# A gated tile moved ahead of the combined activation blocks, and the low half of one weight tile made by VectorE

## The chip, the core and the metric

The kernel runs on one core of a Trainium2 chip. Its time is the device time in microseconds (us) of one execution; less is better. Five engines run side by side: TensorE (PE) multiplies matrices, VectorE (DVE) and ScalarE (ACT) work on tiles, GpSimd (POOL) and SyncE (SP) mostly issue transfers. They keep step by semaphores: an instruction waits until a counter has reached a value, and adds to a counter when it ends. Each engine works through its own list in order.

## The reference

Two layers of an encoder; a token matrix of 512 tokens and 1024 features passes a convolution branch and a state-space branch, is merged and normalised to `h`, and then goes through a gated feed-forward part. The change stands in that part of each layer:

```
h = layer_norm(DEEPNORM_ALPHA * x + merged @ w_o[i], ln1_g[i], ln1_b[i])
g_, u_ = jnp.split(h @ w_gate_up[i], 2, axis=-1)
h2 = layer_norm(DEEPNORM_ALPHA * h + (jax.nn.silu(g_) * u_) @ w_down[i], ln2_g[i], ln2_b[i])
```

`w_gate_up` has 2 x 2816 columns, that is 22 pairs of a gate tile and an up tile of 128 columns; `w_down` brings the 2816 features back to 1024, that is 8 output tiles, each summed over 22 tiles of 128 rows.

## The kernel before

**Two halves of every operand.** Weights and activations are float32. TensorE takes them as a rounded high half and a low half, the rest, and forms three products per tile: high by high, high by low, low by high (`three`, lines 1090 to 1094). `xh` and `xl` (x_hi, x_lo) are the halves of the activations that a stage multiplies, `aah` and `aal` (act_a_hi, act_a_lo) those of the gated tiles 0 to 7, `abh` and `abl` those of the tiles 8 to 15.

**Weight cycles and slots.** Most weights come from one stream in cycles of four tiles of 128x1024, one for each slot (`SLOTS` = 4). A weight tile goes through these steps. SP loads it into one of two raw buffers (`tile`, line 412): slots 0 and 2 share one, slots 1 and 3 the other, so a load waits for `hi_done` of the slot that used the buffer last. ScalarE (`hi`, line 578) copies it to `w_hi`, which rounds it, and writes it with the sign turned to `w_lo`. GpSimd (`lo`, line 469) waits for `hi_done` and issues a transfer that adds the same weights from memory onto `w_lo`, which leaves the weights less the rounded weights, the low half. TensorE (`dense`, line 1100) waits in `slot_ready` for `lo_done` of the slot and for the bank to be free (`evac`), multiplies eight tiles of 128 rows, three products each, into the bank of the slot, and signals `used`. SP, ScalarE and GpSimd handle the tiles in the order of the stream.

**The feed-forward part.** Gated tiles 0 to 3 (`WHOLE` = 4) are made from whole weight tiles, in the two cycles that begin at `C_UP0`: slots 0 and 1 are gate and up of one tile, slots 2 and 3 of the next. For such a tile ScalarE takes the gate's bank with Silu into `sg` (sigmoids), VectorE multiplies it with the up bank into `u` (`swish`, line 2128), ScalarE rounds that into `aah`, VectorE writes the rest into `aal` (`low_act`, line 2136). Tiles 4 to 15 (`UNITS` = 12) are made from 7 smaller products each (`product`, line 1457), a scheme with sums and differences of quarter blocks. It needs four combined blocks of the activations: VectorE forms differences of quarters of the normalised activations (`combine`, line 2072), ScalarE rounds them (`combined_hi`, line 909), VectorE writes the rest (`combined_low`, line 2076). Their weights come from a second array, `w_units`, which SP loads into `z_a` and the raw buffers (`units`, line 417) as soon as the combined blocks have been read out of `z_a` (`t_done`). VectorE and ScalarE make sums of them, and a ring of quarter slots, rounded by ScalarE and completed by GpSimd, holds the rest. Seven products in the order P1, P2, P4, P6, P5, P3, P7 make one tile.

Then the first down cycle (`C_DOWN0`) follows, the whole weight tiles for the down product over gated tiles 0 to 7. Its four tiles are rounded while the last of the 12 units is still being multiplied: ScalarE's `frame` (line 946) calls `hi` for slot 0 behind that unit's first product, and for slots 1 to 3 behind its products P4, P5 and P7.

**Order around the first place.** ScalarE first writes the eight normalised activation tiles (line 906), then rounds the four combined blocks (lines 977 and 978), and then starts gated tile 0 with Silu (line 983) and the two weight tiles of the following cycle. VectorE forms the four differences and the four low halves (lines 2084 to 2092) and then starts `swish` of tile 0 (line 2142 on).

Of the kernel before, what the change touches and what calls it, by code (L numbers as in the profile page):

```python
# [152 lines left out]
def build(nc, x_in, p_in, w_stream, w_units, w_dt, w_ple, par_in, out):  # L153
    ctx = ExitStack()
    with ctx:
# [231 lines left out]
        out_done = sem("out_done")  # L387
        g1_done = sem("g1_done")
# [22 lines left out]
        def _(sp):  # L411
# [36 lines left out]
            for L in range(LAYERS):  # L448
                for first, end, n in ((0 if L else 1, C_DOWN0, WT), (C_DOWN0, C_DOWN2, WT), (C_DOWN2, C_PLE, LAST * P),
                                      (C_PLE, CYCLES, WT)):  # L450
                    if first == C_DOWN0:
                        units(L)
                    with sp.Fori(L * CYCLES + first, L * CYCLES + end) as cyc:
                        for s in range(SLOTS):
                            tile(cyc, s, n)
# [10 lines left out]
        def _(gp):  # L466
# [60 lines left out]
            with gp.Fori(0, LAYERS) as L:  # L527
# [30 lines left out]
                for first, end, n in ((C_GATE_A, C_DOWN0, WT), (C_DOWN0, C_DOWN2, WT), (C_DOWN2, C_PLE, LAST * P), (C_PLE, CYCLES, WT)):  # L558
# [8 lines left out]
                    with gp.Fori(first + (first == C_GATE_A), end) as c:  # L567
# [4 lines left out]
        def _(act):  # L572
# [235 lines left out]
            for L in range(LAYERS):  # L808
# [137 lines left out]
                def frame(n):  # L946
# [3 lines left out]
                    if n < UNITS:  # L950
# [7 lines left out]
                        else:  # L958
                            hi(on(post, C_DOWN0), 0)
# [17 lines left out]
                for i in range(4):  # L977
                    combined_hi(i)
                for f in range(WHOLE):
# [11 lines left out]
                    if not last:  # L991
                        hi(on(c, 1), 2 * r + 1)
                    elif r == 0:
# [92 lines left out]
        def _(pe):  # L1086
# [8 lines left out]

            def slot_ready(cyc, s):
                pe.wait_ge(lo_done[s], 16 * (cyc[0] + 1))
# [14 lines left out]
            def projection(cyc, m, ks=range(4)):  # L1112

                s, h, b = m // 2, m % 2, m % SLOTS
                if ks[0] == 0:
                    pe.wait_ge(lo_done[s], 16 * (cyc[0] + 1))
# [281 lines left out]
            for L in range(LAYERS):  # L1398
# [99 lines left out]
                pe.wait_ge(fl_done, seen(FT * L + KT))  # L1498
                phase(post, C_DOWN0, C_UP2, aah, aal, ready=lambda m: None,
# [25 lines left out]
        def _(dve):  # L1525
            open_(dve, xl_done, dtw_lo, dt_v, ad_ready, turn_ready, grp_ready, conv_done, cb_done,
# [330 lines left out]
            with dve.Fori(0, LAYERS) as L:  # L1857
# [226 lines left out]
                dve.wait_ge(zf_ready, seen(2 * KT * (L + 1)))  # L2084
                combine(0, quadrant(0, 1), quadrant(0, 0))
                dve.wait_ge(t_ready, seen(4 * L + 1))
                combine(1, quadrant(1, 1), combined_sum(0))
                combine(2, quadrant(1, 1), quadrant(0, 1))
                dve.wait_ge(t_ready, seen(4 * L + 2))
                combine(3, quadrant(1, 0), combined_sum(1))  # L2090
                for i in range(4):
                    combined_low(i)

# [48 lines left out]
                for f_ in range(WHOLE):  # L2142
# [32 lines left out]
                for n in range(UNITS + 1):  # L2175
# [13 lines left out]
                    if n > 0:  # L2189
                        low_act(WHOLE + n - 1)  # L2190
                    if n < UNITS:
# [157 lines left out]
```

## Time and profile before

| | |
|---|---|
| median of 3 runs | 2382.52 us (2378.63 to 2385.85) |
| profiled execution | 2385.37 us, its span 2383.5 us |
| TensorE busy | 2328.1 us, 98% of the span |
| VectorE, ScalarE busy | 1666.2 us (70%), 1415.3 us (59%) |
| transfers, share of the 16 DMA engines | 46.4% issued by GpSimd (adding onto `w_lo`), 26.0% issued by SP |
| granted TensorE clock, mean | 0.994 of full speed |

The span runs from the first to the last instruction. Matmuls are pipelined, so TensorE counts as busy while one still drains; a new one starts each 0.23 us with 512 columns at full clock, though each is listed with 0.39 us. A wait is listed with the engine or transfer that ended it. The two layers run the same program: what layer one does near 800 us, layer two does near 1983.

### The profile page before, as it was taken

Reading aid. Unit: us, or ns where it says so; the run is one execution under the profiler, and the core shown is the slowest. Engines: PE = TensorE matmul, PEld = TensorE weight load, DVE = VectorE, ACT = ScalarE, POOL = GpSimd, SP = SyncE. Lnnn points to the kernel's source line nnn. Section 1 sums busy time; section 2 is a strip of 40 time slices with the busy share of each in tenths; the row PEclk is TensorE's granted clock in tenths of the full one; section 3 lists DMA queues with packets and bytes.
Section 4 is the critical chain, followed back from the end, with each engine's and each line's share of the span. In section 5 each row is a group of like instructions: output and inputs, shape, how many; then the busy total and the mean of one; then the engine's idle time right before and its main releaser. Section 6 shows DMA issues by size and latency. Waiting matters only on the chain.

```text
span 2383.5 us, 37119 instructions
## 1 busy us (share of the span) xinstructions
PE 2328.1 (98%) x12312; PEld 1967.9 (83%) x12312; DVE 1666.2 (70%) x2964; ACT 1415.3 (59%) x2439; POOL 493.7 (21%) x581
## 2 busy tenths in 40 slices
PE   8999999999999899999999999999999998999999
PEld 6878888887877799888788888888878777998886
DVE  4899898989545487213758999989895464871147
ACT  5756657376565676444657566664656655763446
POOL 2222222222111122111112122223311111221110
PEclk9999999999999999999999999999999999999999
DMA  7677575857878577988775857747588876778985
GB/s 205 142 167 152 126 176 118 183 131 162 182 182 197 143 182 160 200 205 188 160 160 121 183 126 165 171 108 173 127 177 177 187 184 155 186 166 197 213 188 137
DMA packets 115738, 396.90 MB, mean 167 GB/s; under 512 B 12784, under 2 KB 12784, under 8 KB 115568
## 3 DMA queue, kind: packets, MB, share of 16 engines
q0 software_dynamic: 57600, 188.77, 46.4%
q1 hardware_dynamic: 55728, 200.56, 26.0%
q10 hardware_dynamic: 2240, 5.42, 0.6%
q8 instruction: 93, 1.52, 0.3%
q14 instruction: 77, 0.63, 0.1%
HBM read 392.60 MB, written 2.10 MB: 166 GB/s over the span
## 4 chain that ended last, share of the span: by engine, by line
PE 78%; ACT 8%; DVE 7%; DMA 3%; issue 3%; POOL 1%; POOLq 0%; DVEq 0%; SPq 0%; ACTq 0%
PE bank L1092 21%; PE bank L1094 21%; PE bank L1093 21%; DMA w_lo<-w_stream 3%; PE bank L1134 2%; PE bank L1135 2%; PE bank L1137 2%; ACT decay L635 2%; PE bank L1211 1%; ACT w_lo L584 1%; ACT w_hi L583 1%; PE bank L1217 1%; DVE tmp_m L1657 1%; ACT y_hi L656 1%; PE bank L1229 1%
## 5 line engine op out<-in xcount | busy, mean ns | idle before, releaser
L1092 PE MATMUL bank<-x_hi,w_hi 128*128 128x512 f32 (+1 forms) x1632 | 621.2, 381 | 18.8 <-DMA w_lo<-w_stream 18.8
L1094 PE MATMUL bank<-x_hi,w_lo 128*128 128x512 f32 (+1 forms) x1632 | 608.1, 373 | 0.0
L1093 PE MATMUL bank<-x_lo,w_hi 128*128 128x512 f32 (+1 forms) x1632 | 607.5, 372 | 0.0
L474 POOL DMA_DIRECT2D w_lo<-w_stream x328 | 281.6, 858 | 1438.4 <-ACT w_lo L584 1376.4
L583 ACT ACTIVATE w_hi<-w_raw 128x1024 fp32r<-128x1024 f32 (+1 forms) x330 | 350.1, 1061 | 284.9 <-PE bank L1094 246.0
L1092 PEld LDWEIGHTS bank<-x_hi,w_hi 128*128 128x128 f32 x1632 | 309.4, 190 | 74.0 <-DMA w_lo<-w_stream 20.4
L1094 PEld LDWEIGHTS bank<-x_hi,w_lo 128*128 128x128 f32 x1632 | 309.1, 189 | 54.6
L1093 PEld LDWEIGHTS bank<-x_lo,w_hi 128*128 128x128 f32 x1632 | 309.6, 190 | 53.5 <-issue 3.3
L584 ACT ACTIVATE w_lo<-w_raw 128x1024 fp32r<-128x1024 f32 (+1 forms) x330 | 347.4, 1053 | 0.0
L1570 DVE SCALAR_TENSOR_TENSOR z_a<-glu_out,params,z_a 128x497 f32<-128x497 f32 (+14 forms) x480 | 321.0, 747 | 0.0
L1092 PE MATMUL bank<-act_a_hi,w_hi 128*128 128x512 f32 x480 | 190.2, 396 | 7.8 <-DMA w_lo<-w_stream 4.5
L1094 PE MATMUL bank<-act_a_hi,w_lo 128*128 128x512 f32 x480 | 187.6, 391 | 0.0
L1093 PE MATMUL bank<-act_a_lo,w_hi 128*128 128x512 f32 x480 | 187.5, 391 | 0.0
L1570 DVE SCALAR_TENSOR_TENSOR xs_b_c<-conv_in,params,xs_b_c 128x510 f32<-128x510 f32 (+1 forms) x256 | 184.2, 790 | 0.0
L1134 PE MATMUL bank<-w_hi,x_hi 128*128 128x256 f32 x512 | 153.0, 299 | 1.6 <-DMA w_lo<-w_stream 1.2
L483 POOL TENSOR_SCALAR_AFFINE_SELECT seg_rhs<-steps_split 128x512 fp32r<-128x512 f32 x128 | 130.4, 1099 | 94.7 <-PE bank L1181 94.7
L1135 PE MATMUL bank<-w_lo,x_hi 128*128 128x256 f32 x512 | 144.8, 283 | 0.0
L1137 PE MATMUL bank<-w_hi,x_lo 128*128 128x256 f32 x496 | 140.4, 283 | 0.0
L635 ACT ACTIVATE decay<-bank,steps 128x64 f32<-128x64 f32 x512 | 115.0, 407 | 0.2
L1092 PEld LDWEIGHTS bank<-act_a_hi,w_hi 128*128 128x128 f32 x480 | 90.5, 189 | 29.4 <-DVE act_a_lo L1713 4.1
L651 ACT ACTIVATE squares<-y_tok 128x257 f32<-128x257 f32 x64 | 26.8, 419 | 135.7 <-DVE y_tok L1691 135.7
L1093 PEld LDWEIGHTS bank<-act_a_lo,w_hi 128*128 128x128 f32 x480 | 90.4, 188 | 20.0 <-issue 1.4
(302 smaller groups left out, 4537.3 us busy)
## 6 DMA issues: line engine op xcount, KB each, us to landing
w_raw<-w_stream SPq DMA_DIRECT2D x314, 512.0 KB, 5.1
w_lo<-w_stream POOLq DMA_DIRECT2D x312, 512.0 KB, 7.6
w_lo<-w_units POOLq DMA_DIRECT2D x72, 256.0 KB, 5.3
z_a<-w_units SPq DMA_DIRECT2D x32, 512.0 KB, 4.5
w_raw<-w_units SPq DMA_DIRECT2D x16, 512.0 KB, 4.5
w_raw<-w_stream SPq DMA_DIRECT2D x16, 384.0 KB, 3.8
w_lo<-w_stream POOLq DMA_DIRECT2D x16, 384.0 KB, 6.2
z_b<-x_in SPq DMA_DIRECT2D x4, 512.0 KB, 6.2
```

Of the source, the lines that this page charges most:

```text
L474: gp.dma_start(wlo[:, s, 0:n], w_stream[cyc, s, :, 0:n].bitcast(F32R), accum_op=ALU.add).then_inc(lo_done[s], 16)
L483: gp.affine_select(out=rhs[:, part], in_=ad, compare_op=ALU.is_ge, fill=0.0, base=-1, pattern=[[0, 2 * HG], [-2, HB]], channel_multiplier= ...
L583: act.activation(whi[:, s, 0:n], raw[:, s % 2, 0:n], ACT.Copy)
L584: act.activation(wlo[:, s, 0:n], raw[:, s % 2, 0:n], ACT.Copy, scale=-1.0).then_inc(hi_done[s], 1)
L635: i = act.activation(E[:, c, h, t], quarters(bank[4 + c % 2])[:, h, t], ACT.Exp, bias=of(EDGE, half, c, g)[:, h:h + 1])
L1092: pe.matmul(dst, wh, mh, start=first, stop=False)
L1093: pe.matmul(dst, wh, ml, start=False, stop=False)
L1094: return pe.matmul(dst, wl, mh, start=False, stop=last)
L1134: pe.matmul(dst, xh[:, k, t], h, start=k == 0, stop=False)
L1135: pe.matmul(dst, xh[:, k, t], l, start=False, stop=False)
L1137: pe.matmul(dst, xl[:, k, t], h, start=False, stop=end)
L1570: q = dve.scalar_tensor_tensor(out=outs[i][:, a:b], in0=ins[i][:, a + o:b + o], scalar=w[:, k:k + 1], in1=outs[i][:, a:b], op0=ALU.mult, o ...
```

## The change

Two edits. The first moves work in the order of ScalarE and VectorE. On VectorE `swish` of gated tile 0 stands ahead of the four combined blocks, and its `low_act` between their differences and their low halves. On ScalarE the Silu of gated tile 0, its rounding and the weight tiles of slots 0 and 1 of the next cycle stand ahead of the rounding of the combined blocks. The second takes slot 0 of the first down cycle out of the usual path: ScalarE only writes `w_hi`, and VectorE subtracts it from the raw weights into `w_lo` and signals the new semaphore `low_by_vector`. GpSimd issues no transfer for that slot, SP loads slot 2 of that cycle only after the signal, since it overwrites the raw buffer that VectorE reads, and TensorE waits for the signal and counts one transfer less on slot 0 from there on (`vector_made`). The diff (the line that opens the semaphore for VectorE is left out):

```diff
@@ -385,6 +385,7 @@
         product_done = sem("product_done")
         kept = sem("kept")
         out_done = sem("out_done")
+        low_by_vector = sem("low_by_vector")
         g1_done = sem("g1_done")
         g2_done = sem("g2_done")
         u_ready = sem("u_ready")
@@ -450,7 +451,13 @@
                                       (C_PLE, CYCLES, WT)):
                     if first == C_DOWN0:
                         units(L)
-                    with sp.Fori(L * CYCLES + first, L * CYCLES + end) as cyc:
+                        cyc = L * CYCLES + C_DOWN0
+                        tile(cyc, 0)
+                        tile(cyc, 1)
+                        sp.wait_ge(low_by_vector, seen(L + 1))
+                        tile(cyc, 2)
+                        tile(cyc, 3)
+                    with sp.Fori(L * CYCLES + first + (first == C_DOWN0), L * CYCLES + end) as cyc:
                         for s in range(SLOTS):
                             tile(cyc, s, n)
             tile(ALL_CYCLES, 0)
@@ -564,7 +571,8 @@
                             t, h = {"P1": (1, 0), "P2": (1, 1), "P4": (0, 1)}[p]
                             gp.dma_start(part(wlo, q), w_units[L * UNITS + u_, t, :, h * HALF:(h + 1) * HALF].bitcast(F32R),
                                          accum_op=ALU.add).then_inc(ring_lo[q], 16)
-                    with gp.Fori(first + (first == C_GATE_A), end) as c:
+                        lo(base + C_DOWN0, 1, 2, 3)
+                    with gp.Fori(first + (first in (C_GATE_A, C_DOWN0)), end) as c:
                         lo(base + c, 0, 1, 2, 3, n=n)
 
 
@@ -956,7 +964,9 @@
                             ringed(n + 1, "P2")
                             ringed(n + 1, "P4")
                         else:
-                            hi(on(post, C_DOWN0), 0)
+                            act.wait_ge(raw_ready[0], (base[0] + C_DOWN0 + 1) * 16)
+                            act.wait_ge(used[0], seen(post[1] + C_DOWN0))
+                            act.activation(whi[:, 0, :], raw[:, 0, :], ACT.Copy).then_inc(hi_done[0], 1)
                         sum_hi(n, "S3")
                     if n > 0:
                         unit_hi(n - 1)
@@ -974,8 +984,6 @@
                         after(n, "P7")
                         hi(on(post, C_DOWN0), 3)
 
-                for i in range(4):
-                    combined_hi(i)
                 for f in range(WHOLE):
                     r = f % 2
                     c = on(post, C_UP0 + f // 2)
@@ -990,6 +998,9 @@
                     act.activation(aah[:, f, :], u[:, r, :], ACT.Copy).then_inc(fh_done, 1)
                     if not last:
                         hi(on(c, 1), 2 * r + 1)
+                        if f == 0:
+                            for i in range(4):
+                                combined_hi(i)
                     elif r == 0:
                         ringed(0, "P1")
                         ringed(0, "P2")
@@ -1093,8 +1104,14 @@
                 pe.matmul(dst, wh, ml, start=False, stop=False)
                 return pe.matmul(dst, wl, mh, start=False, stop=last)
 
+            vector_made = [0]
+
+            def transferred(cyc, s):
+
+                return 16 * (cyc[0] + 1 - (vector_made[0] if s == 0 else 0))
+
             def slot_ready(cyc, s):
-                pe.wait_ge(lo_done[s], 16 * (cyc[0] + 1))
+                pe.wait_ge(lo_done[s], transferred(cyc, s))
                 pe.wait_ge(evac[s], seen(cyc[1]))
 
             def dense(cyc, s, mh, ml, nk=KT, ks=None):
@@ -1113,7 +1130,7 @@
 
                 s, h, b = m // 2, m % 2, m % SLOTS
                 if ks[0] == 0:
-                    pe.wait_ge(lo_done[s], 16 * (cyc[0] + 1))
+                    pe.wait_ge(lo_done[s], transferred(cyc, s))
                     pe.wait_ge(evac[b], seen(cyc[1] + m // SLOTS))
                 for k in ks:
                     w = slice(h * HALF + k * P, h * HALF + (k + 1) * P)
@@ -1496,6 +1513,8 @@
                         product(n, p)
                 pe.wait_ge(out_done, seen(len(OUTS) * UNITS * (L + 1) - 3))
                 pe.wait_ge(fl_done, seen(FT * L + KT))
+                pe.wait_ge(low_by_vector, seen(L + 1))
+                vector_made[0] += 1
                 phase(post, C_DOWN0, C_UP2, aah, aal, ready=lambda m: None,
                       held=lambda: pe.wait_ge(out_done, seen(len(OUTS) * UNITS * (L + 1))))
                 phase(post, C_UP2, C_DOWN1, xh, xl)
@@ -2081,16 +2100,6 @@
                 def quadrant(a, t):
                     return za[:, 4 * a:4 * a + 4, t * HT:(t + 1) * HT]
 
-                dve.wait_ge(zf_ready, seen(2 * KT * (L + 1)))
-                combine(0, quadrant(0, 1), quadrant(0, 0))
-                dve.wait_ge(t_ready, seen(4 * L + 1))
-                combine(1, quadrant(1, 1), combined_sum(0))
-                combine(2, quadrant(1, 1), quadrant(0, 1))
-                dve.wait_ge(t_ready, seen(4 * L + 2))
-                combine(3, quadrant(1, 0), combined_sum(1))
-                for i in range(4):
-                    combined_low(i)
-
                 def after(n, p):
                     dve.wait_ge(product_done, seen(PRODUCTS * L + products_until(n, p)))
 
@@ -2139,7 +2148,18 @@
                     hi_, lo_ = ((aah, aal), (abh, abl))[f_ // KT]
                     rest(lo_[:, f_ % KT, :], u[:, f_ % 2, :], hi_[:, f_ % KT, :], fl_done)
 
-                for f_ in range(WHOLE):
+                swish(0, post + C_UP0)
+                dve.wait_ge(zf_ready, seen(2 * KT * (L + 1)))
+                combine(0, quadrant(0, 1), quadrant(0, 0))
+                dve.wait_ge(t_ready, seen(4 * L + 1))
+                combine(1, quadrant(1, 1), combined_sum(0))
+                combine(2, quadrant(1, 1), quadrant(0, 1))
+                dve.wait_ge(t_ready, seen(4 * L + 2))
+                combine(3, quadrant(1, 0), combined_sum(1))
+                low_act(0)
+                for i in range(4):
+                    combined_low(i)
+                for f_ in range(1, WHOLE):
                     if f_ == WHOLE - 1:
                         sums(0, "S1", "S2")
                         sum_low(0, "S1")
@@ -2188,6 +2208,10 @@
                         sum_low(n, "S4")
                     if n > 0:
                         low_act(WHOLE + n - 1)
+                    if n == UNITS - 1:
+                        dve.wait_ge(hi_done[0], seen(L * CYCLES + C_DOWN0 + 1))
+                        dve.tensor_tensor(wlo[:, 0, :], raw[:, 0, :], whi[:, 0, :].bitcast(F32),
+                                          ALU.subtract).then_inc(low_by_vector, 1)
                     if n < UNITS:
                         out(n, "b", un[:, 0:HT], un[:, 0:HT], "P6")
                         sum_low(n, "S3")
```

ScalarE in layer one, before the change, from the normalised activations (`z_a<-z_a`) on; `h_combined_a` and `h_combined_b` are the combined blocks, `sigmoids<-bank` the Silu of a gate, `act_a_hi` the rounded gated tile:

```order
L906 ACTIVATE z_a<-z_a,params 128x512 [waits xl_done] x8
L912 ACTIVATE h_combined_a<-z_b 128x1024 [waits t_ready] x2
L912 ACTIVATE h_combined_b<-h_sums 128x1024 [waits t_ready] x2
L589 ACTIVATE sigmoids<-bank 128x512 [waits used0]
L583 ACTIVATE w_hi<-w_raw 128x1024 [waits used0,raw_ready0]
L584 ACTIVATE w_lo<-w_raw 128x1024
L990 ACTIVATE act_a_hi<-glu_out 128x512 [waits evac1]
L583 ACTIVATE w_hi<-w_raw 128x1024 [waits used1,raw_ready1]
L584 ACTIVATE w_lo<-w_raw 128x1024
L589 ACTIVATE sigmoids<-bank 128x512 [waits used2]
```

The same place after the change (the new kernel's lines are 8 higher here):

```order
L914 ACTIVATE z_a<-z_a,params 128x512 [waits xl_done] x8
L597 ACTIVATE sigmoids<-bank 128x512 [waits used0]
L591 ACTIVATE w_hi<-w_raw 128x1024 [waits used0,raw_ready0]
L592 ACTIVATE w_lo<-w_raw 128x1024
L998 ACTIVATE act_a_hi<-glu_out 128x512 [waits evac1]
L591 ACTIVATE w_hi<-w_raw 128x1024 [waits used1,raw_ready1]
L592 ACTIVATE w_lo<-w_raw 128x1024
L920 ACTIVATE h_combined_a<-z_b 128x1024 [waits t_ready] x2
L920 ACTIVATE h_combined_b<-h_sums 128x1024 [waits t_ready] x2
L597 ACTIVATE sigmoids<-bank 128x512 [waits used2]
```

The Silu of gated tile 0, the weight tiles of slots 0 and 1 and the rounded gated tile have passed the four roundings of the combined blocks.

VectorE in the last unit of layer one, before the change, from C11 of that unit (`rstd<-glu_out,bank`) to its addition for P6 and the low half of S3; `act_b_lo` is the low half of the gated tile before:

```order
L2156 TENSOR_TENSOR rstd<-glu_out,bank 128x256 [waits product_done]
L2125 TENSOR_TENSOR w_lo<-w_sums,w_hi 128x512 [waits s_hi]
L2138 REGISTER_ALU
L1713 TENSOR_TENSOR act_b_lo<-glu_out,act_b_hi 128x512 [waits fh_done]
L2095 REGISTER_ALU
L2156 TENSOR_TENSOR glu_out<-glu_out,bank 128x256 [waits product_done]
L2122 REGISTER_ALU
L2125 TENSOR_TENSOR w_lo<-w_sums,w_hi 128x512 [waits s_hi]
```

The same place after the change:

```order
L2176 TENSOR_TENSOR rstd<-glu_out,bank 128x256 [waits product_done]
L2134 TENSOR_TENSOR w_lo<-w_sums,w_hi 128x512 [waits s_hi]
L2147 REGISTER_ALU
L1732 TENSOR_TENSOR act_b_lo<-glu_out,act_b_hi 128x512 [waits fh_done]
L2212 ISA
L2213 TENSOR_TENSOR w_lo<-w_raw,w_hi 128x1024 [waits hi_done0]
L2104 REGISTER_ALU
L2176 TENSOR_TENSOR glu_out<-glu_out,bank 128x256 [waits product_done]
L2131 REGISTER_ALU
L2134 TENSOR_TENSOR w_lo<-w_sums,w_hi 128x512 [waits s_hi]
```

The subtraction for the down tile stands between the low half of the gated tile and the addition for P6, and waits for `hi_done` of slot 0 (rows without a tile only set a register or wait).

SP behind the last loads of units in layer one, after the change (before it, these four loads were the first turn of a loop, with the waits for `hi_done` alone):

```order
L435 DMA z_a<-w_units 128x1024
L416 DMA w_raw<-w_stream 128x1024 [waits hi_done2,ring_done,s_sum]
L416 DMA w_raw<-w_stream 128x1024 [waits hi_done3]
L416 DMA w_raw<-w_stream 128x1024 [waits hi_done0,low_by_vector]
L416 DMA w_raw<-w_stream 128x1024 [waits hi_done1]
```

The third load, for slot 2, has the new wait, and the fourth stands behind it.

## Rows read from the trace of the kernel before

**Rows 1.** The page: chain that ended last, shares of the span by engine.

```profile
PE 78%; ACT 8%; DVE 7%; DMA 3%; issue 3%; POOL 1%; POOLq 0%; DVEq 0%; SPq 0%; ACTq 0%
```

**Rows 2.** Waits of TensorE, whole span: total us, times, longest us.

```profile
PE bank L1092 <- DMA w_lo<-w_stream: 23.3, 7, 8.4
```

**Rows 3.** Timeline, TensorE, first place, layers one and two: start, us, [idle before].

```profile
805.00 0.79 PE L1092 MATMUL bank<-x_hi,w_hi 128*128 128x512 f32 x1 [8.11 <-DMA w_lo<-w_stream]
...
1988.66 0.80 PE L1092 MATMUL bank<-x_hi,w_hi 128*128 128x512 f32 x1 [8.44 <-DMA w_lo<-w_stream]
```

**Rows 4.** Timeline, TensorE: last product's first matmul, first down matmul, its like in layer two.

```profile
948.92 0.28 PE L1092 MATMUL bank<-h_combined_b,w_hi 128*128 128x256 f32 x1
...
952.78 0.47 PE L1092 MATMUL bank<-act_a_hi,w_hi 128*128 128x512 f32 x1 [2.26 <-DMA w_lo<-w_stream]
...
2136.36 0.47 PE L1092 MATMUL bank<-act_a_hi,w_hi 128*128 128x512 f32 x1 [1.81 <-DMA w_lo<-w_stream]
```

**Rows 5.** Chain of waits, first place, layer one: start, us, what.

```profile
794.59 0.58 ACT sigmoids L589
...
797.76 7.19 DMA w_lo<-w_stream
...
810.75 0.23 PE bank L1093
```

**Rows 6.** Timeline, ScalarE, first place, layers one and two.

```profile
783.80 5.00 ACT L906 ACTIVATE z_a<-z_a,params 128x512 f32<-128x512 f32 x8
...
1967.14 5.00 ACT L906 ACTIVATE z_a<-z_a,params 128x512 f32<-128x512 f32 x8
```

**Rows 7.** Windows: us, busy PE, PEld, DVE, ACT, POOL, clock, DMA share, GB/s.

```profile
796.70:829.50 32.80, 24.69 (x98) 20.06 (x98) 7.57 (x11) 14.92 (x23) 6.84 (x8) 0.84 0.88 219
805.00:811.00 6.00, 6.00 (x15) 4.75 (x16) 0.00 (x0) 2.00 (x2) 1.15 (x2) 0.55 0.97 268
```

**Rows 8.** Chain of waits, first place, layer two.

```profile
1981.11 7.51 DMA w_lo<-w_stream
...
1995.00 0.23 PE bank L1094
```

**Rows 9.** Chain of waits around the first down tile, layer one.

```profile
943.26 0.95 ACT w_lo L584
...
944.91 7.63 DMA w_lo<-w_stream
...
957.35 0.23 PE bank L1092
```

**Rows 10.** Timeline, VectorE, first place, layer one.

```profile
795.77 2.35 DVE L2079 TENSOR_TENSOR h_combined_b<-h_sums,h_combined_b 128x1024 fp32r<-128x1024 f32 x2
```

**Rows 11.** DMA issues of 804 to 805: KB each, us to landing.

```profile
w_lo<-w_stream POOLq DMA_DIRECT2D x1, 512.0 KB, 11.4
```

**Rows 12.** Timeline, GpSimd, first place, layer one.

```profile
797.76 0.86 POOL L474 DMA_DIRECT2D w_lo<-w_stream  x1 [23.85 <-ACT w_lo L584]
...
809.66 0.85 POOL L474 DMA_DIRECT2D w_lo<-w_stream  x1 [4.36 <-ACT w_lo L584]
```

**Rows 13.** Timeline, VectorE, last unit of layer one.

```profile
945.27 0.69 DVE L1713 TENSOR_TENSOR act_b_lo<-glu_out,act_b_hi 128x512 fp32r<-128x512 f32 x1 [0.64 <-ACT act_b_hi L944]
...
946.58 0.69 DVE L2125 TENSOR_TENSOR w_lo<-w_sums,w_hi 128x512 fp32r<-128x512 f32 x1
```

**Rows 14.** DMA issues from 944, from 948 and from 950.5, one us or so each.

```profile
w_raw<-w_stream SPq DMA_DIRECT2D x1, 512.0 KB, 3.7
...
w_lo<-w_stream POOLq DMA_DIRECT2D x1, 512.0 KB, 8.8
...
w_raw<-w_stream SPq DMA_DIRECT2D x1, 512.0 KB, 9.4
```

**Rows 15.** DMA busy tenths, 930 to 975 in 40 slices of 1.1 us.

```profile
DMA  8108899980000399798999999887979999787799
```

**Rows 16.** Timeline, ScalarE, slot 1 of the first down cycle, layer one.

```profile
946.40 1.04 ACT L584 ACTIVATE w_lo<-w_raw 128x1024 fp32r<-128x1024 f32 x1
```

More of the change, by code:

```diff
@@ L1525, in _ @@
         def _(dve):
-            open_(dve, xl_done, dtw_lo, dt_v, ad_ready, turn_ready, grp_ready, conv_done, cb_done,
+            open_(dve, low_by_vector, xl_done, dtw_lo, dt_v, ad_ready, turn_ready, grp_ready, conv_done, cb_done,
                   xw_ready, h_ready, m_ready, yd_read, yp_read, yg_ready, yn_ready, yl_done,
```

## The prediction

> **What bounds the kernel now.** I read first the chain of waits by engine [rows 1]: 78% of the span is TensorE work, so a microsecond counts only where TensorE stands still or runs slowly. Then the waits of TensorE [rows 2]: the largest entry is the accumulating transfers into `w_lo`, 23.3 us in 7 waits. Four of these seven stand at the two places that the change touches. In the first layer TensorE starts a weight tile at 805.00 after 8.11 us of idling, so from 796.9; in the second layer it idles 8.44 us before 1988.66 [rows 3]. After the last product of the piecewise gated tiles it idles 2.26 us before the first down tile in layer one and 1.81 in layer two [rows 4].
>
> Next the chain of waits that ends at 805.00 [rows 5]. Read backwards: the transfer into `w_lo` takes 7.19 us from 797.76 to its landing, before it ScalarE makes both halves of that tile, before that it evacuates the bank with Silu at 794.59, and before that it serves VectorE's combined blocks. ScalarE had ended the normalised activations (8 instructions from 783.80, 5.00 us) at 788.80 [rows 6]. The bank was full by then: TensorE worked on slots 2 and 3, 48 matmuls of 0.23 us, until 796.9, so slots 0 and 1, which come first, ended at about 785.9.
>
> The clock is part of the price. The 13 matmuls from 805.00 to 810.75 take 5.75 us, where 13 at 0.23 take 3.0: 2.8 us lost [rows 3, 5]. The granted clock is 0.55 over 805 to 811, mostly the lower level (1.2 of 2.4 GHz), after the idle time [rows 7]. In layer two 14 matmuls take from 1988.66 to 1995.00, 6.3 instead of 3.2: 3.1 lost [rows 8]. The 2.26 us wait also ends in a slow stretch: 12 matmuls from 952.78 to 957.35 take 4.6 instead of 2.8, 1.8 lost [rows 9]. After the 1.81 us wait I count no such loss.
>
> **First edit: gated tile 0 and its weights ahead of the combined blocks.** ScalarE's Silu moves from 794.59 to 788.80. From Silu to the issue of the transfer it is 797.76 - 794.59 = 3.17 us [rows 5], all of it ScalarE's work on a tile loaded long before and GpSimd's issue. So the issue comes at 791.97, and with the 7.24 us from issue to first matmul TensorE starts at 799.21 instead of 805.00: 5.8 us earlier, 2.3 us of idling left. Layer two: activations end at 1967.14 + 5.00 = 1972.14 [rows 6], issue at 1975.31, landing 7.51 later, first matmul at 1982.86 instead of 1988.66 [rows 8]: 5.8 earlier, 2.6 left. Together 11.6 us.
>
> The clock after the shorter gap is not shown; its bounds are no loss (gain 2.8 + 3.1 = 5.9) and the old loss (gain 0). I take the nearest row, the 2.26 us gap that cost 1.8, in both layers: gain 5.9 - 3.6 = 2.3.
>
> What pays for it: VectorE runs one product ahead of the four differences and one low half behind them; ScalarE rounds two weight tiles ahead of the four blocks. By my estimate ScalarE ends its second tile at 793.6 (788.8, Silu and act rounding 0.5 each, two tiles of 1.9), the blocks 4.2 later, and VectorE's last low half, 1.2 us each [rows 10], ends near 800 instead of 798.1. Who waits for it: SP's loads of the first piecewise tile. They also stand behind the raw load for slot 3, which waits for slot 1's rounding, and that now ends earlier, so they go out near 800, no later than before. The products that read the blocks start only after two more gated tiles, near 822. The cost is 0; if that cover were gone it would be these 2 us per layer.
>
> Slots 1 and 2 behind slot 0: slot 1's transfer is issued about 794.3 and wanted 5.5 us after 799.2, 10.4 us later. Slot 2's goes out near 801.0 (797.8, Silu 0.5, tile 1.9, issue 0.7) and is wanted at 810.2, or at 812 with a slow clock. Transfers of this stretch landed in 7.19 to 11.4 us [rows 5, 11], so slot 2 may add 0 to 2.2 us per layer. I take 0, since a slow clock moves the need back.
>
> The Trainium skill (GPSIMD Engine Reference, Specifications) says that GpSimd's SBUF interfaces are shared with VectorE and contend with VectorE instructions that have two SBUF inputs. That speaks against this edit, because VectorE's differences now run just when GpSimd issues slot 0's transfer. The rows bear no price out: the issue at 797.76 took 0.86 us while VectorE ran its two-input low halves, the one at 809.66 took 0.85 [rows 12, 10]. By the rows the sum stays; by the rule each such issue would be longer by an unknown part.
>
> **Second edit: low half of down tile 0 by VectorE.** Removed: 0.95 us of ScalarE and a 512 KB transfer with its 7.63 us landing [rows 9]. Added: one VectorE subtraction of 128x1024, 1.2 us like the low halves of that size [rows 10], right behind the low half at 945.27 (0.69 us) [rows 13]. It ends near 947.2, and TensorE's last product at 950.5. Queued behind it on VectorE: the addition for P6, then S3's low half (was 946.58 to 947.27, now up to 948.2), which the last product wants at 948.92 [rows 4]; 0.7 us are left, so 0. The wait of 2.26 and 1.81 us goes (4.1), and layer one's slow clock with it (1.8).
>
> What is late next: slot 2. Its raw load overwrites slot 0's buffer, so SP holds it until VectorE's subtraction, 947.2, where it could go at 944.2; slot 3's load stands behind it on SP. A raw load lands in 3.7 us nearly alone and 9.4 beside others [rows 14]; ScalarE's halves take 1.9, the issue 0.7, the transfer 7.6 to 8.8 [rows 9, 14]. So slot 2 is ready between 961.1 and 968.0. TensorE wants it two slots of 5.5 us after 950.5, at 961.5: a wait of 0 to 6.5 us, and up to 3 for the clock. The DMA engines stand idle here from about 940 to 944.6 [rows 15], and with slot 0's transfer gone nothing is under way when these loads start; I go by the short row, with 0.5 us per layer for the company of slot 1's transfer. Slot 1: its halves ended at 947.44 [rows 16], its transfer is issued near 947.4 to 948.1, lands 7.6 later at 955.0 to 955.7 (956.9 by the longer row), wanted at 956.0: inside the same 0.5. Net 4.1 + 1.8 - 1.0 = 4.9.
>
> **Sum.** 11.6 + 2.3 + 4.9 = 18.8 us. The profiled execution took 2385.37 us (span 2383.5 and 1.9 around it), so 2366.6; it lies 2.85 above the median of the three runs, 2382.52, which gives 2363.7, forecast 2364.
>
> **Rivals.**
> 1. The clock holds over the gaps of 2.3 and 2.6 us. For it: the 1.81 us gap did not drop it. Against: the 2.26 us gap did. Gain 22.4, time 2360.
> 2. The wait of the second edit only moves to slots 1 and 2 and nothing is won there. For: the held raw load, and the 9.4 us row. Against: the idle DMA engines. Gain 13.9, time 2368.6.
> 3. The DMA engines hold the end of the first stretch. From 796.7 to 829.5 they were busy 0.88 of 32.8 us, 28.9 us of work [rows 7]. The new stretch, from 792.0 to the first product near 822.7, is 30.7 us; a share of 0.94 is wanted, and 0.97 was reached from 805 to 811. If 0.88 is all they give, 2.1 us per layer are lost, time 2368; if the first product stays at 829.5, only 4.9 remains, 2377.6.
> 4. Slower: the raw load held for VectorE comes so late that slot 2 costs more than both places give. With the longest rows, 9.4 for the load and 11.4 for the transfer, slot 2 is ready at 947.2 + 9.4 + 2.6 + 11.4 = 970.6, a wait of 9.1 and 3 for the clock, 24.2 in two layers, against 5.9 removed there and 13.9 at the first place: 4.4 slower, 2387. It decides from 9.9 us per layer on. Against it: those two rows come from stretches in which several transfers run together.
>
> **How the numbers follow.** Chances: forecast 0.50, rival 1 0.20, rival 2 0.16, rival 3 0.10 (mostly its small form), rival 4 0.04. A measurement of this kernel can tell about 0.3%, 7.1 us. The first three cases and the small form of rival 3 gain more: faster 0.91. The full rival 3 and half of rival 4 are no change: 0.07. Slower, the worse half of rival 4: 0.02. The range goes from rival 1 without the 1.0 us of new waits, 2359, less 2 us for the spread of the runs, to rival 2 with 2.2 us lost at slot 2 of the first stretch in one layer and the same spread: 2357 to 2373.
>
> **What would show it.** Right: Silu stands directly behind the activations, the wait there is 2 to 3 us in each layer, the slow stretch behind it is about 8 matmuls or none, and the wait before the first down tile is gone. Wrong: a wait on `w_lo` before the third slot of the down tiles that is longer than 2 us; first products that wait for their own transfers; loads of the piecewise tiles later than before against the start of TensorE's stretch; a last product that waits for S3's low half.

## The result and the profile after

The changed kernel takes 2365.46 us (median of 4 runs, 2363.03 to 2369.58), the kernel before on the same chip 2381.84 (4 runs, 2378.63 to 2385.85): a ratio of 0.9932, 95% interval 0.9911 to 0.9953, so 16.4 us won with an interval of 11 to 21. The profiled execution took 2363.03 us with a span of 2361.4; before it was 2385.37 and 2383.5. Between the two profiled spans lie 22.1 us. This pair is further apart than the medians, and the account below is of this pair.

Waits of TensorE over the whole span of the changed kernel: total us, times, longest us.

```profile
PE bank L1246 <- DVE y_tok L1717: 9.9, 8, 1.2
PE bank L1103 <- DMA w_lo<-w_stream: 9.0, 6, 2.8
```

The entry that led with 23.3 us in 7 waits [rows 2] is now second with 9.0 in 6, and its longest wait, 2.8, is the one at the program's start. What is left at the two places stands in the timeline of TensorE, layer one and layer two each:

```profile
798.64 0.80 PE L1103 MATMUL bank<-x_hi,w_hi 128*128 128x512 f32 x1 [2.51 <-DMA w_lo<-w_stream]
...
1970.74 0.50 PE L1103 MATMUL bank<-x_hi,w_hi 128*128 128x512 f32 x1 [2.42 <-DMA w_lo<-w_stream]
...
943.07 0.40 PE L1103 MATMUL bank<-act_a_hi,w_hi 128*128 128x512 f32 x1
...
954.79 0.50 PE L1103 MATMUL bank<-act_a_hi,w_hi 128*128 128x512 f32 x1 [0.65 <-DMA w_lo<-w_stream]
...
2125.04 0.50 PE L1103 MATMUL bank<-act_a_hi,w_hi 128*128 128x512 f32 x1 [0.26 <-DMA w_lo<-w_stream]
```

The first two rows answer to [rows 3]: 8.11 and 8.44 us of idling have become 2.51 and 2.42. The third answers to [rows 4]: the first down tile now starts with no wait behind it. Two slots later there is a small new one, 0.65 and 0.26.

The chain of waits of the changed kernel around the first place answers to [rows 5]:

```profile
784.88 3.16 ACT z_a L914 x5
788.04 0.48 ACT sigmoids L597
788.52 0.78 ACT w_hi L591
789.37 1.06 ACT w_lo L592
...
791.13 7.47 DMA w_lo<-w_stream
...
798.64 0.80 PE bank L1103
...
802.32 0.23 PE bank L1105
```

The transfer goes out at 791.13 instead of 797.76 and needs 7.47 us where it needed 7.19. VectorE's and ScalarE's combined blocks are gone from this chain; ScalarE's activations, its work on the tile and the landing are what is left. From 798.64 to 802.32 there are 8 matmuls in 3.68 us, where 8 at 0.23 take 1.84: 1.8 lost to the lower clock (granted 0.51 there, by a window shown below), against 2.8 before. In layer two, where 3.1 were lost [rows 8], the clock holds (last section).

The account of the pair. First place, layer one: wait 8.11 to 2.51, 5.6, and clock 2.8 to 1.8, 1.0. Layer two: wait 8.44 to 2.42, 6.0, and clock 3.1 to 0.3, 2.8. Down tile, layer one: wait 2.26 and clock 1.8 against 0.65 now, 3.4. Layer two: 1.81 against 0.26, 1.55. Together 20.4 of 22.1 us. Of the rest 0.8 lies ahead of the first place already: TensorE's idling began at 805.00 - 8.11 = 796.89 before [rows 3] and begins at 798.64 - 2.51 = 796.13 now; 0.9 is spread over the rest of the program.

### The profile page after: what moved, and what is told of

It is laid out like the page before. It is cut to its first block, busy times and chain, and to the rows that moved or that the text cites. A ratio compares the mean times of both kernels' runs of the same rounds, so it can differ in the third digit from the quotient of the medians.

```text
span 2361.4 us, 37100 instructions
## 1 busy us (share of the span) xinstructions
PE 2320.0 (98%) x12312; PEld 1962.2 (83%) x12312; DVE 1670.1 (71%) x2966; ACT 1412.7 (60%) x2437; POOL 478.4 (20%) x579
## 4 chain that ended last, share of the span: by engine, by line
PE 78%; ACT 8%; DVE 7%; DMA 4%; issue 2%; DVEq 0%; POOLq 0%; SPq 0%; ACTq 0%
PE bank L1103 21%; PE bank L1105 21%; PE bank L1104 21%; DMA w_lo<-w_stream 3%; PE bank L1151 3%; PE bank L1152 3%; PE bank L1154 3%; ACT decay L643 2%; PE bank L1228 1%; ACT w_lo L592 1%; PE bank L1234 1%; ACT w_hi L591 1%; DMA w_raw<-w_stream 1%; DVE tmp_m L1676 1%; ACT y_hi L664 1%
## 5 line engine op out<-in xcount | busy, mean ns | idle before, releaser
L490 POOL TENSOR_SCALAR_AFFINE_SELECT seg_rhs<-steps_split 128x512 fp32r<-128x512 f32 x128 | 115.9, 989 | 92.2 <-PE bank L1198 92.2
```

The source lines that it names most:

```text
L490: gp.affine_select(out=rhs[:, part], in_=ad, compare_op=ALU.is_ge, fill=0.0, base=-1, pattern=[[0, 2 * HG], [-2, HB]], channel_multiplier= ...
```

## Experiments

The theory: each microsecond comes from an earlier transfer into `w_lo` at one of the two places; the edits act apart from one another; the late combined blocks cost nothing, since two gated tiles cover them. The rivals: the gain comes from one edit alone, or the lateness is paid somewhere else. Two groups of kernels ran, each beside the kernel before on the same chip: medians 2381.80 us (15 runs) and 2383.77 us (9 runs).

**The first edit alone.** The kernel before with the moves on ScalarE and VectorE, without the low half by VectorE:

```diff
@@ ScalarE @@
-                for i in range(4):
-                    combined_hi(i)
...
+                        if f == 0:
+                            for i in range(4):
+                                combined_hi(i)
@@ VectorE @@
+                swish(0, post + C_UP0)
+                dve.wait_ge(zf_ready, seen(2 * KT * (L + 1)))
...
+                low_act(0)
...
```

> The first edit alone, on the kernel before. Theory (the two edits act at separate places and add up): the wait before the first tile of the second gated cycle is 2.4 to 2.6 us in each layer instead of 8.11 and 8.44; the waits before the first down tile stay at 2.3 and 1.8 us; 12 to 17 us faster than before, ratio 0.993 to 0.995. Rival (the DMA engines hold the end of this stretch): the first product of the piecewise tiles starts no earlier against the start of the stretch's wait, and the time is within 5 us of before.

Measured: 2366.67 us (2364.0 to 2371.61), ratio 0.9937 (0.9924 to 0.9951), 15.1 us won. Timeline of TensorE, the first place and the first down tile in both layers:

```profile
798.36 0.80 PE L1093 MATMUL bank<-x_hi,w_hi 128*128 128x512 f32 x1 [3.89 <-DMA w_lo<-w_stream]
...
1974.00 0.50 PE L1093 MATMUL bank<-x_hi,w_hi 128*128 128x512 f32 x1 [2.34 <-DMA w_lo<-w_stream]
...
945.86 0.47 PE L1093 MATMUL bank<-act_a_hi,w_hi 128*128 128x512 f32 x1 [1.97 <-DMA w_lo<-w_stream]
...
2120.98 0.50 PE L1093 MATMUL bank<-act_a_hi,w_hi 128*128 128x512 f32 x1 [2.39 <-DMA w_lo<-w_stream]
```

The wait at the first place shrinks, the one at the down tile stays. Layer one's 3.89 is longer than expected and than in the changed kernel because that one transfer took 8.81 us to land (from 789.50) and not 7.47.

**The second edit alone.** The changed kernel with the first edit taken back:

```diff
@@ ScalarE @@
+                for i in range(4):
+                    combined_hi(i)
...
-                        if f == 0:
-                            for i in range(4):
-                                combined_hi(i)
@@ VectorE @@
-                swish(0, post + C_UP0)
                 dve.wait_ge(zf_ready, seen(2 * KT * (L + 1)))
...
-                low_act(0)
                 for i in range(4):
                     combined_low(i)
-                for f_ in range(1, WHOLE):
+                for f_ in range(WHOLE):
```

> The second edit alone, on the kernel before. Theory (the wait ahead of down slot 0 goes, a smaller one of 0.3 to 0.7 us comes back at slot 2 because its raw load is held): 3 to 5 us faster, ratio 0.998 to 0.9985; the first place keeps its 8.1 and 8.4 us. Rival (the wait only moves to slots 1 and 2): waits of 2 us or more there and no gain.

Measured: 2377.57 us (2375.91 to 2380.28), ratio 0.9983 (0.9974 to 0.9992), 4.2 us won. Timeline of TensorE, first place and third down tile of layer one, third down tile of layer two:

```profile
804.72 0.80 PE L1102 MATMUL bank<-x_hi,w_hi 128*128 128x512 f32 x1 [8.14 <-DMA w_lo<-w_stream]
...
961.08 0.50 PE L1102 MATMUL bank<-act_a_hi,w_hi 128*128 128x512 f32 x1 [0.48 <-DMA w_lo<-w_stream]
...
2139.58 0.50 PE L1102 MATMUL bank<-act_a_hi,w_hi 128*128 128x512 f32 x1 [0.25 <-DMA w_lo<-w_stream]
```

The first place is as before, the down place as in the changed kernel. In the waits the two edits act apart. In the times 15.1 + 4.2 = 19.3 stands against the 16.3 that both give in this group (next); with intervals of 11.7 to 18.1, 1.9 to 6.2 and 12.9 to 19.3 a shared part of some 3 us is neither shown nor excluded.

**The changed kernel again**, with no edit, to see how far two executions of one program differ.

> The changed kernel again, beside its two halves on the same chip. If the edits add up, its gain is the sum of the gains of the first and the second edit alone, within 4 us: 15 to 20 us, ratio 0.992 to 0.994. If they share a gain (the earlier first place already removes the wait before the down tiles, or the reverse), it is smaller than that sum by the shared part.

Measured: 2365.51 us (2362.42 to 2367.94), ratio 0.9932 (0.9919 to 0.9946). Waits at the first place 2.59 and 1.91, at the third down tile 0.6 in both layers. The clock fell after 2.59 and held after 1.91.

**Silu among the activations.** If what is left at the first place is ScalarE's turn, Silu of gated tile 0 and slot 0's rounding can go between the fourth and the fifth normalised activation, 2.5 us earlier:

```diff
                 for m in range(KT):
+                    if m == 4:
+                        take(on(post, C_UP0), 0, sg[:, :], ACT.Silu)
+                        hi(on(post, C_UP0 + 1), 0)
                     act.wait_ge(xl_done, seen(KT * k + m + 1))
...
-                    take(c, 2 * r, sg[:, :], ACT.Silu)
+                    if f > 0:
+                        take(c, 2 * r, sg[:, :], ACT.Silu)
...
```

> The changed kernel, with Silu of gated tile 0 and the rounding of slot 0's weights moved further ahead, between the fourth and the fifth normalised activation of ScalarE, where the bank is just full. Theory (what is left of the wait, 2.51 and 2.42 us, is only ScalarE's remaining activations ahead of Silu): the issue of the transfer comes 2.3 to 2.5 us earlier, the wait is 0 to 0.3 us in both layers, no slow stretch follows it, the combined blocks end up to 1.5 us later and nobody waits for them: 5 to 7 us faster than the changed kernel, ratio to before 0.990 to 0.991. Rival (the DMA engines are now the bound of the stretch, busy 0.95 of it): the wait returns at slot 2 of the stretch or at the first product, 1 to 3 us per layer, and the time stays within 3 us of the changed kernel.

Measured: 2358.43 us (2356.19 to 2364.14), ratio 0.9911 (0.9897 to 0.9924). Timeline of ScalarE, then of TensorE (all its waits at the first place in both layers), then GpSimd's last issue before the second of them:

```profile
781.81 2.55 ACT L917 ACTIVATE z_a<-z_a,params 128x512 f32<-128x512 f32 x4
784.26 0.57 ACT L597 ACTIVATE sigmoids<-bank 128x512 f32<-128x512 f32 x1
...
786.63 2.55 ACT L917 ACTIVATE z_a<-z_a,params 128x512 f32<-128x512 f32 x4
```

```profile
800.89 0.50 PE L1108 MATMUL bank<-x_hi,w_hi 128*128 128x512 f32 x1 [0.43 <-DMA w_lo<-w_stream]
...
1980.50 0.50 PE L1108 MATMUL bank<-x_hi,w_hi 128*128 128x512 f32 x1 [0.54 <-DMA w_lo<-w_stream]
```

```profile
1971.40 0.85 POOL L481 DMA_DIRECT2D w_lo<-w_stream  x1 [3.55 <-ACT w_lo L592]
```

Slot 0 has no wait any more. So the 2.4 to 2.6 us of the changed kernel were ScalarE's order too. Half a microsecond is left, in layer one at slot 1; in layer two it is slot 3, whose transfer, the fourth and last of the cycle, goes out at 1971.40 and lands at 1980.46. The kernel is 7.1 us faster than the changed one in its group. The same kernel in the second group:

> The kernel with Silu and slot 0 among the activations once more, beside its two variants on the same chip: ratio to before 0.990 to 0.992, the two variants 0 to 3 us faster than this.

Measured: 2359.57 us (2358.18 to 2360.73), ratio 0.9899 (0.9884 to 0.9914); waits at the first place 0.58 (slot 3) and 0.33 (slot 2), and 1.55 at the third down tile of layer two.

**VectorE's subtraction made twice.** The held raw load was the step of the second edit that I priced least surely. Doubling the subtraction moves the signal that lets it go 1.2 us back:

```diff
                         dve.wait_ge(hi_done[0], seen(L * CYCLES + C_DOWN0 + 1))
+                        step(dve.tensor_tensor(wlo[:, 0, :], raw[:, 0, :], whi[:, 0, :].bitcast(F32), ALU.subtract))
+                        dve.wait_ge(dve_order, issued())
                         dve.tensor_tensor(wlo[:, 0, :], raw[:, 0, :], whi[:, 0, :].bitcast(F32),
                                           ALU.subtract).then_inc(low_by_vector, 1)
```

> The changed kernel, with VectorE's subtraction for the down tile made twice, so that the signal for SP comes one subtraction (1.2 us) later and nothing else is added. Theory (slot 2 of the first down cycle waits because its raw load is held until the signal): its wait grows from 0.65 and 0.26 us by 0.9 to 1.4 us per layer, its raw load starts 1.2 us later against the last product; 2 to 3 us slower than the changed kernel, more where the clock falls after it. Rival (slot 2 waits for the crowd of transfers, whenever its raw load starts): the wait stays at 0.3 to 0.7 us. Second rival (VectorE's chain in the last unit has no slack left): the last product waits for the low half of S3.

Measured: 2366.27 us (2363.09 to 2370.62), ratio 0.9923 (0.9908 to 0.9938), not to be told from the changed kernel. The wait at the third down tile is 0.18 in layer one, with 0.39 at the second, and 0.80 in layer two: a miss, since it fell in one layer and grew by 0.54 in the other, where 0.9 to 1.4 was expected in both. Timelines of the steps for slot 2 in layer one (VectorE, SP, ScalarE) and the transfer from the chain of waits, of this kernel and then of the changed one:

```profile
941.75 1.23 DVE L2215 TENSOR_TENSOR w_lo<-w_raw,w_hi 128x1024 fp32r<-128x1024 f32 x1
943.00 0.33 SPq L416 DMA_DIRECT2D w_raw<-w_stream  x1
947.22 1.06 ACT L591 ACTIVATE w_hi<-w_raw 128x1024 fp32r<-128x1024 f32 x1 [5.05 <-issue]
...
949.93 7.64 DMA w_lo<-w_stream
```

```profile
937.85 1.22 DVE L2213 TENSOR_TENSOR w_lo<-w_raw,w_hi 128x1024 fp32r<-128x1024 f32 x1
939.10 0.33 SPq L416 DMA_DIRECT2D w_raw<-w_stream  x1
943.26 1.07 ACT L591 ACTIVATE w_hi<-w_raw 128x1024 fp32r<-128x1024 f32 x1 [3.74 <-PE bank L1105]
...
945.97 8.78 DMA w_lo<-w_stream
```

The steps follow one another as I had claimed: subtraction, held load, ScalarE's halves, transfer. The held load lands 4.1 us after its issue in both kernels (DMA issues of the profile), and ScalarE begins right then, though its rows name another releaser or none. (The profile's own chain of waits puts another load here, 939.54 to 944.81 in the changed kernel. That is slot 3's, which waits for slot 1's rounding: ScalarE's work on slot 2 had begun before it landed.) The first down tile starts at 945.73 here and at 943.07 in the changed kernel, so against it the subtraction ends 1.25 us later (2.75 ahead, 4.00 there), the transfer goes out 1.3 later (4.20 behind, 2.90 there), and it takes 1.14 less. In layer two it takes 1.09 less, 7.65 against 8.74. So the signal does move the transfer, and a shorter landing takes up most of the lateness. In the ten layers of the five executions with one subtraction at this place this transfer took 7.9 to 9.9 us, so that 7.64 and 7.65 lie below them all; why is not shown.

**Silu among the activations, and the subtraction earlier.** The other side of the same test: the subtraction directly behind the multiply-out of the last unit (C11), ahead of two other pieces of work:

```diff
                         out(n, "C11", gn[:, 0:HT], un[:, 0:HT], "P2")
+                        if n == UNITS - 1:
+                            dve.wait_ge(hi_done[0], seen(L * CYCLES + C_DOWN0 + 1))
+                            dve.tensor_tensor(wlo[:, 0, :], raw[:, 0, :], whi[:, 0, :].bitcast(F32),
+                                              ALU.subtract).then_inc(low_by_vector, 1)
                         sum_low(n, "S4")
...
-                    if n == UNITS - 1:
-                        dve.wait_ge(hi_done[0], seen(L * CYCLES + C_DOWN0 + 1))
...
```

> The kernel with Silu and slot 0 among the activations, with VectorE's subtraction also moved up, directly behind C11 of the last unit. Theory: the raw load of slot 2 starts 1.0 to 1.3 us earlier against the last product, the wait of slot 2 in the down cycle falls to 0 to 0.2 us in both layers, and the last products do not wait for VectorE; 0.5 to 2 us faster than without the move, ratio to before 0.989 to 0.991. Rival (crowd of transfers): the wait of slot 2 stays at 0.3 us or more.

Measured: 2358.46 us (2355.71 to 2360.6), ratio 0.9898 (0.9883 to 0.9913). The subtraction in VectorE's timeline, and the only wait of TensorE in the first down cycles of both layers:

```profile
931.97 1.21 DVE L2215 TENSOR_TENSOR w_lo<-w_raw,w_hi 128x1024 fp32r<-128x1024 f32 x1
```

```profile
944.22 0.47 PE L1108 MATMUL bank<-act_a_hi,w_hi 128*128 128x512 f32 x1 [0.20 <-issue]
```

The subtraction ends 5.2 us ahead of the first down tile (938.39) instead of 4.0, and slot 2 is not waited for; the 0.20 us are slot 1's, whose transfer lands at 944.13. One execution would not settle it, since slot 2 was without a wait also in layer one of both kernels with Silu alone moved. But counted from the start of the first down tile, TensorE is ready for slot 2 near 11.1 us; the transfer lands at 8.2 to 9.8 in the four layers with the early subtraction (this kernel and the next) and at 10.3 to 12.6 in the ten layers just named, eight of which wait. So the small new wait comes from the held load; how long it is hangs on the landing of the transfer as well. In the time the move is not to be told from the kernel without it (2358.46 and 2359.57 in one group).

**Slot 1's rounding among the activations too.** The cover of the combined blocks put to the test: on top of the kernel just told, slot 1's rounding stands ahead of the last two activations, and VectorE's differences, which want all eight, start later.

```diff
+                    if m == 6:
+                        hi(on(post, C_UP0 + 1), 1)
                     act.wait_ge(xl_done, seen(KT * k + m + 1))
...
-                        hi(on(c, 1), 2 * r + 1)
                         if f == 0:
                             for i in range(4):
                                 combined_hi(i)
+                        else:
+                            hi(on(c, 1), 2 * r + 1)
```

> As the one before, with the weights of slot 1 too rounded among the activations, ahead of the last two. Theory: the waits of 0.43 and 0.54 us that were left at slot 1 of the second gated cycle go; the combined blocks come about 0.5 to 2 us later, and since the products that read them start more than 15 us later, nothing waits for them; 0 to 2 us faster than the one before. Rival (the combined blocks or the loads of the piecewise tiles behind them have no slack left): a wait of 1 us or more before the first product, and slower.

Measured: 2361.88 us (2358.78 to 2364.87), ratio 0.9911 (0.9897 to 0.9924): a miss. The median gives back 3.4 us of the kernel it was built on; the two intervals overlap, so the waits have to show the loss. Timeline of this kernel, VectorE, then GpSimd's issue of slot 3, then TensorE at slot 3 in both layers:

```profile
792.57 1.23 DVE L2101 TENSOR_TENSOR z_b<-z_a 128x1024 f32<-128x1024 f32 x1 [5.55 <-ACT z_a L919]
...
802.38 0.69 DVE L2151 TENSOR_TENSOR glu_out<-bank,sigmoids 128x512 f32<-128x512 f32 x1
```

```profile
806.34 0.85 POOL L481 DMA_DIRECT2D w_lo<-w_stream  x1 [3.88 <-ACT w_lo L592]
```

```profile
815.76 0.50 PE L1111 MATMUL bank<-x_hi,w_hi 128*128 128x512 f32 x1 [2.50 <-DMA w_lo<-w_stream]
...
1984.99 0.79 PE L1111 MATMUL bank<-x_hi,w_hi 128*128 128x512 f32 x1 [2.37 <-DMA w_lo<-w_stream]
```

Both are waits of slot 3 (one of 0.29, at slot 2 of layer one, is left out); the kernel it was built on has 0.82 and 0.21 at slot 3. My expectation had taken layer two's 0.54 for slot 1's, but it was slot 3's already. The rounding of slot 3 on ScalarE stands behind its rounding of gated tile 1, this behind VectorE's product for that tile, and this, in VectorE's order, behind the four differences and the four low halves. With Silu alone moved the same rows read 789.22, 799.03 and, for the issue, 802.98; here all are 3.4 us later (2 us of slot 1's rounding and 1.4 by which the whole stretch starts later in this execution). In the kernel with Silu alone moved, slot 3's transfer lands at 802.98 + 9.19 = 812.17 and TensorE, done with slot 2 at 811.9, starts on it at once; in layer two TensorE waits 0.54 for it. So nothing was left to spare there, and the 2 us by which the combined blocks come later are paid at slot 3.

## Why the prediction was right

The forecast was 2364 us against 2365.46 measured; the gain 18.8 against a median of 16.4 (11 to 21). Alone, the first edit gave 15.1 where 13.9 was forecast and the second 4.2 where 4.9 was; no run shows which term makes both together 2.4 less than forecast, which the interval allows. By its own steps:

- **First edit, the start.** 11.6 us forecast, 5.6 + 6.0 = 11.6 in the profile; idle time left 2.3 and 2.6 forecast, 2.51 and 2.42 seen. Silu stands directly behind the activations, at 787.95 by the timeline of ScalarE.
- **The clock after the shorter gap.** I took the loss of 1.8 in both layers, a gain of 2.3 between bounds of 0 and 5.9. It came in layer one (1.8) and not in layer two (0.3): 3.8 won in this pair. This is the term that was mis-sized there. Rival 1, that it holds, was half true, and by chance: in the first edit alone it fell in both layers.
- **The late combined blocks at no cost.** True for this order. VectorE's last low half ends at 799.06 (forecast near 800), and the first product starts at 822.12 (forecast 822.7):

```profile
796.71 2.35 DVE L2098 TENSOR_TENSOR h_combined_b<-h_sums,h_combined_b 128x1024 fp32r<-128x1024 f32 x2
```

```profile
822.12 0.28 PE L1103 MATMUL bank<-x_hi,w_hi 128*128 128x256 f32 x1
```

  SP's loads of the first piecewise tile go out at 799.09 (801.99 before), so no later. What I had not seen is who else waits for VectorE here: slot 3, by way of gated tile 1. In the changed kernel its transfer is issued at 802.92 and lands 9.9 later, at 812.8, and it is wanted near 817.0 (798.64, three tiles of 24 matmuls at 0.23 and 1.8 for the clock): some 4 us to spare. With Silu among the activations TensorE is there at 811.9 and the landing at 812.17, nothing to spare (and 0.54 short in layer two), and the last experiment went past that.
- **Slots 1 and 2 of the first stretch at 0.** No wait there in the profiled execution, and 0.41 once, at slot 2, in the repeated one.
- **GpSimd's issue beside VectorE's differences.** The issue at 791.13 now runs while VectorE makes its two-input differences (790.42 to 793.83):

```profile
791.13 0.86 POOL L481 DMA_DIRECT2D w_lo<-w_stream  x1 [17.97 <-ACT w_lo L592]
794.26 0.85 POOL L481 DMA_DIRECT2D w_lo<-w_stream  x1 [2.27 <-issue]
```

  0.86 and 0.85 us, as in [rows 12]. Of the prediction's row only the first 0.36 us ran beside VectorE's low halves, which end at 798.12; the issue at 791.13 lies wholly beside the differences, and is the better test. The Trainium skill (GPSIMD Engine Reference, Specifications) states that the SBUF interfaces of GpSimd are shared with VectorE, with contention with VectorE instructions that have two SBUF inputs. The trace shows no price of it in these issues.
- **Second edit.** 4.9 forecast. 4.2 (1.9 to 6.2) measured for it alone, 3.4 + 1.55 = 4.95 in the profile. The wait went, and slot 2 is late next, as said: 0.65 and 0.26 where I allowed 0.5 per layer. The short raw load was the right row: slot 2's took 4.1 us in layer one and 3.7 in layer two, not 9.4.
- **The rivals.** Rival 2 (the wait only moves) needed about 3 us per layer at slots 1 and 2 to give back the 5.9 won there, rival 4 (slower) 9.9; at most 0.8 is seen at slot 2 in the kernels with the order of the change, and 1.55 once with Silu moved. Rival 3 (the DMA engines hold the end) wanted a share of 0.94 that they could not give; they gave it. (Its chances are uneven with its words: 0.91 for faster leaves 0.05 of its 0.10 to the small form, which is half and not most.) Windows of the changed kernel, columns as in [rows 7], the first the stretch that the prediction named, the second the slow matmuls at its first place:

```profile
792.00:822.70 30.70, 28.19 (x120) 22.99 (x119) 12.10 (x15) 16.67 (x24) 6.00 (x7) 0.94 0.95 234
798.60:802.00 3.40, 3.36 (x8) 2.69 (x9) 1.75 (x3) 2.71 (x4) 0.86 (x1) 0.51 1.00 227
```

  The share is 0.95 over those 30.7 us, where it was 0.88 over 32.8 [rows 7], and the first product moved 7.3 us forward, from here:

```profile
829.41 0.28 PE L1092 MATMUL bank<-x_hi,w_hi 128*128 128x256 f32 x1
```

The best version is not the changed kernel but the one with Silu among the activations: ratios of 0.9911 and 0.9899, with the earlier subtraction 0.9898.

## What to carry to other kernels

Follow a wait on a transfer back to the engine that prepares it and ask what stands ahead of that work in program order only by habit: here moving Silu, a rounding and two weight tiles ahead of the combined blocks gave 15 us, and moving Silu and the first of those tiles 2.5 us further gave 7 more. Before an engine's work is put off, list all that is queued behind it, including what returns through another engine: VectorE's last low half of the combined blocks had 23 us of cover at the products that read it and, by way of gated tile 1, only 4 us at slot 3, which the next step used up. A term for the clock after a gap of about 2 us is best put as a chance, not as a number.

## What the hardware showed that was not expected

Whether TensorE's clock falls to its lower level after a gap is not settled by the gap's length between 1.8 and 2.9 us. At the two places it fell after 1.97, 2.34 and 2.39 (first edit alone), 2.26 (before), 2.37 (both slots among the activations), 2.51 (changed) and 2.59 (changed again); it held after 1.81 (before), 1.91 (changed again), 2.42 (changed) and 2.50 (both slots). After 3.06, 3.89 and 4.30 it fell. The wait for `w_lo` at the program's start says the same more strongly: the clock fell after 1.89 (subtraction twice), 2.09 (before) and 2.29 (both slots), and held after 2.85 (changed). Two gaps of nearly one length, timeline of TensorE, the first edit alone in layer two's down tile and the changed kernel at layer two's first place:

```profile
2121.28 0.62 PE L1094 MATMUL bank<-act_a_lo,w_hi 128*128 128x512 f32 x1
2121.70 0.63 PE L1095 MATMUL bank<-act_a_hi,w_lo 128*128 128x512 f32 x1
2122.13 0.63 PE L1093 MATMUL bank<-act_a_hi,w_hi 128*128 128x512 f32 x1
```

```profile
1971.08 0.39 PE L1104 MATMUL bank<-x_lo,w_hi 128*128 128x512 f32 x1
1971.30 0.40 PE L1105 MATMUL bank<-x_hi,w_lo 128*128 128x512 f32 x1
1971.54 0.40 PE L1103 MATMUL bank<-x_hi,w_hi 128*128 128x512 f32 x1
```

After 2.39 us a matmul starts each 0.43 us, after 2.42 each 0.23. What decides it was not found.

The landing of the first place's transfer in layer one spread from 7.19 us (before) over 7.47 (changed) and 8.81 (first edit alone) to 9.26 (subtraction twice), at one place of nearly one program. That alone is 2 us of idle time. Runs of one kernel spread by 2.5 to 8 us; how much of that such landings make is not shown, and their cause stays open.
